# Hybrid decoder trunk on one core: near tokens' forms kept on the chip, values split in the attention stage, results stored from their sum tiles

## What is computed

```python
h = rms_norm(x, norm_g[l])
proj = jnp.einsum('bsd,de->bse', h, w_in[l])
u_pool, z_pool, q, k, v, z_attn, gate_logits = jnp.split(proj, splits, axis=-1)
y_pool = multiscale_pool(u_pool, pool_w[l], pool_scale[l]) * jax.nn.silu(z_pool)
attn = stick_breaking_attention(q, k, v)     # A[t,s] = beta[t,s] * prod_{s<j<t} (1 - beta[t,j])
y_attn = attn.reshape(B, S, ATTN_WIDTH) * jax.nn.silu(z_attn)
gates = jax.nn.sigmoid(gate_logits + b_gate[l]).reshape(B, S, 2, D)
merged = gates[:, :, 0] * (y_pool @ w_pool_up[l]) + gates[:, :, 1] * (y_attn @ w_attn_up[l])
x = x + merged @ w_out[l]
return rms_norm(x, final_g)
```

## Time and profile before

| | us |
|---|---|
| median of 3 runs | 1717.15 (1713.16 to 1722.72) |
| the profiled execution | 1719.18 |
| its span, first to last instruction | 1717.4 |
| TensorE busy in it | 1609.2 |
| mean granted clock of TensorE | 0.977 of full speed |

### The profile page before, as it was taken

The page is one execution under the profiler, slowest core; times in us unless marked ns, Lnnn a source line. Parts: engine busy times, 40 slices in busy tenths (PEclk is TensorE's granted clock), DMA queues, the critical chain, the costliest instruction groups (busy, mean ns, idle before and its releaser), DMA issues. The chain is left out here.

```text
span 1717.4 us, 24997 instructions
## 1 busy us (share of the span) xinstructions
PE 1609.2 (94%) x8030; PEld 1333.7 (78%) x8030; DVE 1140.0 (66%) x1554; ACT 752.9 (44%) x1432; POOL 870.0 (51%) x633
## 2 busy tenths in 40 slices
PE   8999998887699999899998999999999899999998
PEld 6878876665588888688877888877888678888886
DVE  6737326871288979788887988888888674242423
ACT  4412223331255766466665666665666442111111
POOL 3521115551267766677766776778666341505040
PEclk9999999998899999899999999999999999999999
DMA  7743268898723425244297432433423583535331
GB/s 256 222 151 139 75 205 272 298 319 259 275 75 102 117 82 147 67 121 108 66 296 262 120 108 77 145 93 95 112 83 100 181 245 132 159 110 158 111 98 73
DMA packets 164692, 262.38 MB, mean 153 GB/s; under 512 B 48465, under 2 KB 73553, under 8 KB 164578
## 3 DMA queue, kind: packets, MB, share of 16 engines
q1 hardware_dynamic: 164578, 260.98, 48.7%
HBM read 166.54 MB, written 94.37 MB: 152 GB/s over the span
## 5 line engine op out<-in xcount | busy, mean ns | idle before, releaser
L1573 DVE TENSOR_TENSOR_SCAN left<-keep,left 128x512 f32<-128x512 f32 x192 | 294.6, 1534 | 40.7 <-issue 31.4
L1642 POOL TENSOR_TENSOR ring<-raw,ring 128x512 fp32r<-128x512 f32 x138 | 229.0, 1660 | 120.1 <-ACT ring L1489 107.6
L1409 PE MATMUL psum<-hT,ring 128*128 128x512 f32 x644 | 265.1, 412 | 9.8 <-DVE sum_d L1611 6.3
L1413 PE MATMUL psum<-hT,ring 128*128 128x512 f32 x644 | 263.7, 410 | 0.0
L1411 PE MATMUL psum<-hT,ring 128*128 128x512 f32 x644 | 262.8, 408 | 0.0
L1495 ACT ACTIVATE keep<-psum 128x512 f32<-128x512 f32 (+3 forms) x320 | 170.6, 533 | 184.2 <-PE psum L1435 182.2
L1502 ACT ACTIVATE wt<-psum 128x512 fp32r<-128x512 f32 (+3 forms) x320 | 170.9, 534 | 108.7 <-PE psum L1443 106.3
L1443 PE MATMUL psum<-ident,left 128*128 128x128 f32 x1088 | 172.2, 274 | 29.5 <-DVE wt L1579 29.4
L1455 PEld LDWEIGHTS psum<-wt,vm 128*128 128x128 f32 x1088 | 172.2, 190 | 31.2 <-issue 6.1
L1579 DVE TENSOR_TENSOR wt<-psum,wt 128x512 fp32r<-128x512 f32 (+3 forms) x320 | 189.9, 593 | 8.4 <-ACT wt L1502 5.9
L73 PE MATMUL psum<-hT,w_parts 128*128 128x512 f32 x392 | 158.5, 404 | 38.1 <-DVE store_lo L849 31.3
(11 more groups left out here) (159 smaller groups left out, 3194.6 us busy)
## 6 DMA issues: line engine op xcount, KB each, us to landing
raw<-in_w_strips SPq DMA_DIRECT2D x92, 256.0 KB, 4.2
hT<-form_scratch SPq DMA_DIRECT2D x44, 512.0 KB, 7.5
form_scratch<-t_parts SPq DMA_DIRECT2D x32, 512.0 KB, 6.1
qm<-qk_scratch SPq DMA_DIRECT2D x128, 128.0 KB, 4.3
gate_scratch<-staging SPq DMA_DIRECT2D x64, 256.0 KB, 4.0
gate<-gate_scratch SPq DMA_DIRECT2D x64, 256.0 KB, 4.0
xt<-in_x SPq DMA_DIRECT2D x16, 512.0 KB, 5.2
xT<-in_x_T SPq DMA_DIRECT2D x16, 512.0 KB, 4.1
```

The lines of the kernel that those rows point to most:

```text
L1409: pe.matmul(o, hi, m_hi, start=k == 0, stop=False)
L1413: last = pe.matmul(o, lo, m_hi, start=False, stop=k == HK - 1)
L1573: dve.tensor_tensor_scan(left[:, n % LN, span][:, ::-1], k, k, carry, ALU.mult, ALU.bypass).then_inc(scanned, 1)
L1642: pool.tensor_tensor(out_, a, b, op).then_inc(s, 1)
```

## The change

**Forms.** In strips 6 and 7 the far half (tokens 1024 to 2047) is formed, rounded and stored as before. In strips 8 and 9 the near half is formed by the same VectorE operations into a new tile `t_near` (4 forms x 4 x 512), with no rounding and no store. When TensorE has done the last unit that reads a block (11, 2 or 3), ScalarE rounds `t_near` into hT's blocks 4 to 7 (`form_near`) and VectorE writes the low parts (`near_low`), beside units (10,0), (10,1), (11,0) and (11,1). No near form goes to HBM or comes back.

**Values.** `V_SLOTS` is gone. A value unit (512 keys of one head) is loaded twice from v, shifted by one, into one pair of buffers (`v_raw`, `v_prev`, 4 x 64), GpSimd subtracts, ScalarE rounds into `vm`, GpSimd writes the low part into `vm`. Four units are done in strip 9, 28 in stage 3, where the difference stands two steps behind the load and the rounding at least three. The next load waits for the low part. `KN` is 4 instead of 5.

**Results.** A z's sigmoid goes to `res` (one slot of staging), VectorE's product goes into the sum tile, and that tile is stored. A gate's sigmoid is taken in place. The other slot of staging is a fifth sum tile, `sum_e`. Who next writes a sum tile waits for its last store; the sigmoid doesn't.

The diff, cut to its core:

```diff
-    KN, VN, QN = 5, 4, 3
+    KN, VN, QN = 4, 4, 3
...
     def load_v(self, sp, pair, u, e, c):
         cols = slice(pair * P + e * HD, pair * P + (e + 1) * HD)
-        for part in range(2):
-            sp.dma_start(self.vm[:, u % self.VN, :, part * HD:(part + 1) * HD].bitcast(F32),
-                         self.vp_d[part, c * CH:(c + 1) * CH, cols].rearrange("(a q) d -> q a d", q=P)
-                         ).then_inc(self.v_in[u % self.VN], DMA)
+        for raw, at in ((self.v_raw, 1), (self.v_prev, 0)):
+            sp.dma_start(raw[:, :, :], self.v_d[c * CH + at:(c + 1) * CH + at, cols].rearrange("(a q) d -> q a d", q=P)
+                         ).then_inc(self.v_in, DMA)
+
+    def value_diff(self, pool, u):
+        pool.wait_ge(self.v_in, (u + 1) * 2 * DMA)
+        pool.tensor_tensor(self.v_raw[:, :, :], self.v_prev[:, :, :], self.v_raw[:, :, :],
+                           ALU.subtract).then_inc(self.v_diff, 1)
+
+    def value_hi(self, act, u):
+        act.wait_ge(self.v_diff, u + 1)
+        act.activation(self.vm[:, u % self.VN, :, 0:HD], self.v_raw[:, :, :], ACT.Copy).then_inc(self.v_hi, 1)
+
+    def value_lo(self, pool, u):
+        pool.wait_ge(self.v_hi, u + 1)
+        pool.tensor_tensor(self.vm[:, u % self.VN, :, HD:2 * HD], self.v_raw[:, :, :],
+                           self.vm[:, u % self.VN, :, 0:HD].bitcast(F32), ALU.subtract).then_inc(self.v_lo, 1)
...
@@ stage2, SP
-                if (n, c) in V_SLOTS:
-                    t = V_SLOTS.index((n, c))
-                    if t >= 1:
-                        put_v(t - 1)
-                    if t + 1 < TT:
-                        load_v(t + 1)
...
+                    if n == V_STRIP:
+                        if c == 0:
+                            for s in t_stored:
+                                sp.wait_ge(s, HK * DMA)
+                            sp.wait_ge(b_stored, 3 * HK * DMA)
+                        head_loads.load_first_v(sp, c)
             load(STRIPS)
             put_qk(STRIPS - 2, 2)
             put_qk(STRIPS - 2, 3)
-            put_v(TT - 1)
             for i in range(2):
-                sp.wait_ge(v_stored[i], TT * DMA)
                 sp.wait_ge(stored[i], stored_upto[use_of["qk", G + PAIRS + 1, 0] + i])
             head_loads.load_first(sp)
             put_qk(STRIPS - 1, 2)
             put_qk(STRIPS - 1, 3)
...
-            load_t(T2)
...
-            load_t(T1)
...
@@ stage2, ScalarE
+            def form_near(i):
+                act.wait_ge(proj_done, near_after[i % 2] + 1)
+                for kk in range(HK):
+                    act.activation(hT[:, HOME[TURN[i]], kk, 0, :], t_near[:, i, kk, :], ACT.Copy).then_inc(near_hi, 1)
...
+                    if n == V_STRIP and c >= 1:
+                        head_loads.value_hi(act, c - 1)
                 scalar_weights(act, n + 2)
...
+            form_near(2)
+            copy_strip(*units[-5])
+            form_near(0)
+            copy_strip(*units[-4])
             scalar_weights(act, STRIPS)
+            form_near(1)
+            copy_strip(*units[-3])
+            form_near(3)
+            copy_strip(*units[-2])
             scalar_weights(act, STRIPS + 1)
...
@@ stage3, the table of steps
-    V_LOAD = [max(K_LAST[u - VN] + AV_LAG + 1 if u >= VN else 0, K_FIRST[u] - SOON) for u in range(PAIRS * NK)]
+    V_LOAD, V_HI = [], []
+    for u in range(PAIRS * NK):
+        V_LOAD.append(max(K_FIRST[u] - SOON, V_HI[u - 1] + 1) if u >= VN else 0)
+        V_HI.append(max(V_LOAD[u] + 3, K_LAST[u - VN] + AV_LAG + 1) if u >= VN else 0)
...
@@ stage3, SP
-                if s in (-2, -1):
-                    j = (T3, T4)[s + 2]
-                    for kk in range(HK):
-                        sp.dma_start(hT[:, HOME[j], kk, :, :].bitcast(F32), form_d[0, j, kk]).then_inc(form_in[j], DMA)
...
-                sp.dma_start(dst, res[:, k % 2, :]).then_inc(res_stored[k % 2], DMA)
+                sp.dma_start(dst, sums[tile_index(k)]).then_inc(sum_stored[tile_index(k)], DMA)
...
@@ stage3, ScalarE's result
-                wait(act, res_stored[k % 2], k // 2, DMA)
                 if kind(g) < 2:
-                    act.activation(res[:, k % 2, :], source(k), ACT.Sigmoid).then_inc(act_out, 1)
+                    wait(act, silu_done, z_index(k))
+                    act.activation(res, source(k), ACT.Sigmoid).then_inc(act_out, 1)
                 else:
-                    act.activation(res[:, k % 2, :], source(k), ACT.Sigmoid, bias=bcol[:, b:b + 1]).then_inc(act_out, 1)
+                    act.activation(source(k), source(k), ACT.Sigmoid, bias=bcol[:, b:b + 1]).then_inc(act_out, 1)
...
@@ stage3, GpSimd's steps
+                for u in at(V_LOAD, s - 2):
+                    if u >= VN:
+                        value_diff(u)
                 for w in at(W_STEP, s):
                     low_w(w)
+                for u in at(V_HI, s):
+                    if u >= VN:
+                        value_lo(u)
```

267 lines of the change are left out of this document (132 added, 135 removed).

## The result

The changed kernel takes **1678.1 us** (median of 4 runs, 1675.6 to 1680.2) against 1719.0 for the kernel before, measured beside it on the same chip (median of 4, 1713.2 to 1722.7). The ratio is 0.9764, with a 95% interval from 0.9732 to 0.9797. Forecast were 1665 us and a range of 1647 to 1688. The profiled execution took 1680.2 us, 39.0 less than the one of before (1719.2), where the sum said 52.3.

A forecast was written before the change was run, and what follows sets the result against it. TensorE's own work was taken as the floor, its idle time and half clock as the gain. Stage 2's 36.6, the opening's 7.7 and attention's 8 sum to 52.3 us off 1719.2, 1666.9; forecast 1665, range 1647 to 1688.

The forecast's parts named there:

- part 1: Strips 6 to 9: 26.0 us a strip in 6 and 7, no wait in 8 and 9; 8 us left.
- part 3: End of stage 2: the 9.9 us wait for SyncE's late q/k store goes; 0 left, upper end 4.
- part 2: First four values in strip 9: weight strip 11 still waits 3 us, plus 2 for clock and restart; ends 0 and 9.
- parts 3 and 4: End of stage 2: the 9.9 us wait goes; attention's opening without form loads: 7.7 us less, 6.9 of wait stay.
- The results' stores: Attention: ScalarE no longer waits for result stores to leave staging; 16 us gone, clock included.
- part 5: Attention: 16 us gone with result-store waits, 8 added by value work (bounds 0 and 28); net 8 less.
- rival (d): Attention: GpSimd, held by landings, delays y_out at all 28 units; slower above 2.2 us a unit, 1741 at 3; chance 0.04.
- tight places: Attention: value loads wait at seven heads' last units and the form swap; 1 us in six places, 2 in the swap.
- three signs of being wrong: Attention: TensorE waits for GpSimd's vm or km; L1579 late behind ScalarE's value copies; VectorE over 90% busy.
- rival (a): Contention in attention: GpSimd's added operations cost VectorE 29 us, all reaching TensorE; about 1694 us; chance 0.05.
- the rule that speaks against the change: Attention: GpSimd contends with VectorE's instructions with two SBUF inputs; in full, the gain of 52.3 us shrinks to 23.
- Rival (b): Value ring: weight strip 11 and tight places cost double, strips 6 and 7 keep their pace; 1685 us; chance 0.15.

The follow-up runs named there:

- y4: The kernel before without its value work in stage 2 (attention copies values straight from the sums): 1686.7 us, ratio 0.9806.
- x2: x1 with the key ring's fifth slot back, so attention differs from the kernel before in the results' stores alone: 1648.2 us, ratio 0.9598.
- x3: x1 plus 56 GpSimd subtractions at the value work's places, on a tile nobody reads, without waits: 1670.5 us, ratio 0.9717.
- x1: The changed kernel without the value work of attention's 28 units, whose values are copied straight into their ring: 1651.7 us, ratio 0.9608.
- y2: The changed kernel with two tiles for raw values, one still for the row before: 1671.2 us, ratio 0.9717.

## Why the prediction was nearly right, and where it was not

**Strips 6 to 9 (part 1): the pace right, the reserve added to it wrong.** The forecast was a circle of 26.0 us for a strip and a total of 8 us of stall. The rows of L843 around strip 7 of the changed kernel, in the columns of the earlier trace rows; ScalarE's copy released each of them:

```profile
288.04 0.69 DVE L843 TENSOR_TENSOR store_lo<-psum,staging 128x512 fp32r<-128x512 f32 x1 [2.13 <-ACT staging L741]
...
295.05 0.69 DVE L843 TENSOR_TENSOR store_lo<-psum,staging 128x512 fp32r<-128x512 f32 x1 [1.18 <-ACT staging L741]
...
300.50 0.69 DVE L843 TENSOR_TENSOR store_lo<-psum,staging 128x512 fp32r<-128x512 f32 x1 [1.25 <-ACT staging L741]
...
306.41 0.69 DVE L843 TENSOR_TENSOR store_lo<-psum,staging 128x512 fp32r<-128x512 f32 x1 [1.19 <-ACT staging L741]
...
313.89 0.69 DVE L843 TENSOR_TENSOR store_lo<-psum,staging 128x512 fp32r<-128x512 f32 x1 [2.13 <-ACT staging L741]
```

From 288.04 to 313.89 are 25.85 us. Of the 3.4 us that were to go, 1.7 from each odd slot, 3.9 did: chunk 1's slot went from 7.92 to 5.45 and chunk 3's from 8.90 to 7.48, while the even slots of chunks 0 and 2 (6.97 and 5.57) now take 7.01 and 5.91. The waits of TensorE in the whole stretch, to the end of stage 2:

```profile
PE psum L75 <- DVE store_lo L843: 2.9, 3, 1.8
PE psum L75 <- POOL w_parts L806: 0.2, 1, 0.2
```

The circle's own wait was forecast at 4.2 and is 2.9. The other 3.8 of the 8 were a reserve for restarts, half clock and a late store; none came, the granted clock is 1.00. The low end of 26 for the whole stretch left part 3's upper end out: 49.6 less 14, 9 and 4 is 22.6. In strips 8 and 9 the spacing falls to 5.4 (348.58 to 354.02), as forecast.

**Weight strip 11 (part 2): a wait of 0.2 us for a forecast of 3, and no clock lost.** GpSimd's low part was to end 28.4 to 32 us after unit (9,0); it ended after 27.5 (358.94 against 331.43), since from the first issue of a value load to the difference it took 3.0 to 4.2 us, where two issues of 1.1 and a landing of 4.1 from the quiet part of attention had stood in the sum. TensorE wanted it at 27.3. The term was near its edge and fell to the cheap side. Before 257.3, where the forecast's stretch began, another 0.6 us went that I had left out; the value work had begun in strips 4 and 5.

**The end of stage 2 and the opening (parts 3 and 4): right.** No wait near 10 us is left; the weights leave SyncE 8.1 us behind the first mix_t load (405.82 against 397.69), as forecast, 7.7 us are saved, and the wait left is 6.9 us. y4, which drops the values' work and keeps the form loads, has a wait of 15.2 us there (14.6 before), so it wasn't the values' work that held the opening.

**The results' stores: right.** 17.3 us by x2 and before, for 16. No wait of ScalarE for a result's store stands in the changed kernel.

**The value work in attention: the step that failed.** "Nothing in the trace shows this wait", said part 5; the bounds were 0 and 28 us, and I took 8 because the bottleneck had slack before each of ScalarE's waits. It costs 26.4. The error has two halves. First, I asked what GpSimd's new *waits* would do and not what its added *time* does: x3 has none of the waits and costs 18.8 us. The chain that I named, "VectorE's row_sum waits for y_out, and TensorE for row_sum", was the right one, and slower rival (d) was built on it; but the holder is GpSimd's backlog at a head's end, not a landing, and its price is 18.8 / 28 = 0.7 us a unit, under the 2.2 from which (d) would decide. The wait was there to be read, in the trace of the kernel before (VectorE's waits; us, times, longest):

```profile
DVE row_sum L1588 <- POOL y_out L1642: 18.2, 15, 3.2
```

Time put ahead of y_out in GpSimd's order adds to such a wait. Second, the slack of 1.5 to 2 us belongs to ScalarE's queue; VectorE's was a different one, and at the first head's end it was used up, for VectorE stood still there already in x1 (1.79 us at 503.66, 3.95 in x3). The tight places that I did name, the heads' ends, are where the long waits of the changed kernel lie: VectorE's for y_out at 504, 617 and 842 (4.0 to 4.6 us each), TensorE's for query tiles up to 517.5, 630.5, 745.6 and 857.4. A second raw tile takes 7 us of it back (y2). None of the three signs of being wrong came: TensorE waits neither for vm nor for km, VectorE's L1598 (L1579 before) waits 5.0 us for ScalarE where it waited 5.9, and VectorE is busy for 83% of attention. The loss came by two tiles that they didn't name, row_sum and qm.

**Contention (rival (a) and the rule that speaks against the change): it is there, but not where I put it.** The 29 us of VectorE time that L890 against L894 would give don't appear: its scans take 1550 and 1548 ns without and with the 56 operations. Scans are slowed in attention all the same, from 1.26 us to 2.40, and in both kernels alike. The Trainium skill (GPSIMD Engine Reference, Specifications) says that VectorE's instructions with two SBUF inputs contend with GpSimd; the traces agree, in stage 2 and in attention. For the added work it is GpSimd that gives way: its y_out took 0.45 us at 503.43 and 1.16 at 509.45 of the changed kernel, beside a working VectorE, and x3's 56 operations took 57.2 us where 56 x 0.74 = 41 would do without a neighbour. So a part of the backlog is contention; how much of the time lost it makes wasn't measured.

**The range held because two errors offset each other, and that is luck.** Stage 2 gave 9.3 more than its terms (8.7 in the stretch, 0.6 before it) and attention 23 less, of which 18.4 are the value work's, up to 3.5 the key ring's, and the rest lies between single executions. Rival (b), 1685, was nearer in number than the forecast's own case, but by luck too: of its three terms one came, the tight places at more than double, while weight strip 11 cost 0.2 us and strips 6 and 7 did get faster.

## What to carry to other kernels

Before work is added to an engine that isn't the bottleneck, list what stands behind it in its order and is waited for through a single buffer; a wait that already exists there, however hidden, can grow by the added time, and the engine's idle share (GpSimd had 30% of the attention stage free, 266 of 875 us by the earlier trace rows) says nothing of it. Price added work by an idle copy of it: without its waits, on a tile that nobody reads, and once more with the suspected buffer doubled; and look whether the copy keeps the engine busy as long as the work does (57.2 us for 47.8 here). Waits of parallel chains can stand in for each other, so an edit that removes one and gains little may be half of a pair: 3 and 7 us alone, 16 with both and the loads' order.
